# A hybrid attention and mixture-of-experts layer on one core: the shared gather moved between the halves of gate and up, left columns first, fewer steps before the first expert

## What is computed

```
logits = h @ router_w + router_b;  top 4 of 32 per token, softmax over them -> combine
for e in range(32):
    gate = min(h @ w_gate[e] + b_gate[e], 7)
    up   = clip(h @ w_up[e] + b_up[e], -7, 7)
    act  = gate * sigmoid(1.702 * gate) * (up + 1)
    y   += combine[:, e] * (act @ w_down[e] + b_down[e])
x = x + y;  final RMS norm
```

## Time and profile before

| what | value |
|---|---|
| median of three runs | 1249.69 us (1244.88 to 1253.77) |
| profiled execution | 1244.24 us, span 1242.5 us |
| TensorE matmul busy | 1156.3 us, 93% of the span |
| weight loading on TensorE | 606.0 us |
| VectorE, ScalarE, GpSimd busy | 355.5, 224.1, 9.1 us |
| read from HBM | 446.33 MB, 360 GB/s over the span |
| the ring's 384 loads | 128 each of gate, up, down; 26.5 to 26.9 us from issue to landing |

### The profile page before, as it was taken

How to read it: one execution, slowest core, us unless ns; L and a number is a source line. 1 busy time by engine, 2 the same in 40 slices (tenths; PEclk the granted TensorE clock), 3 DMA queues, 4 the chain that set the end, 5 groups by cost and what they waited for, 6 DMA issues and landing times.

```text
span 1242.5 us, 16294 instructions
## 1 busy us (share of the span) xinstructions
PE 1156.3 (93%) x6235; PEld 606.0 (49%) x6235; DVE 355.5 (29%) x768; ACT 224.1 (18%) x389; POOL 9.1 (1%) x16
## 2 busy tenths in 40 slices
PE   7999998898999999999999989898889989898987
PEld 6998998885344343434334333334333434343423
DVE  4446666443213221222221212212121212121212
ACT  5444446432001010101101000001010101010102
POOL 0000000000000000000000000000000000000000
PEclk9999999899999999999999999999999999999999
DMA  9956444568999999999999999999999999999992
GB/s 293 285 171 186 140 139 150 199 245 333 424 421 421 421 421 421 421 421 421 419 420 421 421 421 421 421 421 421 421 420 421 420 422 420 422 421 421 421 418 92
DMA packets 88916, 448.56 MB, mean 361 GB/s; under 512 B 7832, under 2 KB 35790, under 8 KB 39686
## 3 DMA queue, kind: packets, MB, share of 16 engines
q1 hardware_dynamic: 86282, 439.94, 87.3%
q0 software_dynamic: 1472, 5.51, 1.8%
q10 hardware_dynamic: 1084, 2.02, 0.5%
HBM read 446.33 MB, written 1.11 MB: 360 GB/s over the span
## 4 chain that ended last, share of the span: by engine, by line
PE 59%; DMA 37%; issue 1%; DVE 1%; SPq 1%; ACT 1%; ACTq 0%; DVEq 0%
DMA slot<-in_w_up 35%; PE psum L976 19%; PE psum L1005 9%; PE psum L667 5%; PE psum L668 5%; PE psum L669 5%; PE psum L919 4%; PE psum L934 3%; PE psum L942 2%; PE psum L977 2%; PE psum L737 1%; PE psum L772 1%; PE psum L765 1%; SPq L373 1%; PE psum L750 1%
## 5 line engine op out<-in xcount | busy, mean ns | idle before, releaser
L976 PE MATMUL psum<-slot,xT 128*64 128x512 f32 x1024 | 455.8, 597 | 58.0 <-DMA slot<-in_w_up 52.1
L977 PE MATMUL psum<-slot,xT 128*64 128x512 f32 x1024 | 457.2, 598 | 1.5 <-issue 1.5
L976 PEld LDWEIGHTS psum<-slot,xT 128*64 128x64 f32 x1024 | 136.6, 138 | 344.1 <-issue 344.1
L1005 PE MATMUL psum<-slot,guT 128*64 128x512 f32 x1024 | 233.8, 598 | 0.0
L1291 DVE COPY gu<-psum 128x512 f32<-128x512 f32 x32 | 22.1, 691 | 542.0 <-PE psum L977 542.0
L977 PEld LDWEIGHTS psum<-slot,xT 128*64 128x64 f32 x1024 | 136.6, 137 | 15.4 <-issue 15.4
L1005 PEld LDWEIGHTS psum<-slot,guT 128*64 128x64 f32 x1024 | 67.8, 136 | 129.1 <-issue 119.6
L639 ACT COPY gu<-psum 128x512 f32<-128x512 f32 x32 | 18.7, 585 | 466.4 <-PE psum L977 466.4
L1054 DVE TENSOR_TENSOR pieces<-raw,pieces 128x2048 fp32r<-128x2048 f32 x32 | 73.3, 2292 | 72.4 <-ACT pieces L474 72.4
L667 PE MATMUL psum<-hT_hi,pieces 128*128 128x256 f32 x296 | 84.9, 287 | 0.0
L668 PE MATMUL psum<-hT_lo,pieces 128*128 128x256 f32 x296 | 83.9, 284 | 0.0
(11 more groups left out here) (177 smaller groups left out, 945.3 us busy)
## 6 DMA issues: line engine op xcount, KB each, us to landing
slot<-in_w_gate SPq DMA_DIRECT2D x128, 1024.0 KB, 26.5
slot<-in_w_up SPq DMA_DIRECT2D x128, 1024.0 KB, 26.9
slot<-in_w_down SPq DMA_DIRECT2D x128, 1024.0 KB, 26.9
raw<-in_w_in SPq DMA_DIRECT2D x23, 1024.0 KB, 5.4
raw<-in_w_branch_a SPq DMA_DIRECT2D x4, 1024.0 KB, 5.0
raw<-in_w_out SPq DMA_DIRECT2D x4, 1024.0 KB, 4.9
windows<-bias_table POOLq DMA_DIRECT2D x8, 384.0 KB, 4.0
windows<-bias_table POOLq DMA_DIRECT2D x4, 576.0 KB, 7.1
```

The source lines that it names most:

```text
L976: mm(bank(GU + nb)[0:CAP, :], x_k, gate[:, c, cols], start=k == 0, stop=k == KC - 1)
L977: last = mm(bank(GU + nb)[CAP:P, :], x_k, up[:, c, cols], start=k == 0, stop=k == KC - 1)
L1005: last = mm(bank(DOWN)[half * CAP:(half + 1) * CAP, :], hidden[:, k, :], down[:, c, half * BANK:(half + 1) * BANK], start=k == 0, stop=k = ...
```

## The change

Parts, in the order of the program:

1. SyncE waits for `gu_rows_in` before it issues the third portion of expert weights.
2. VectorE no longer clears `y_half` and `spreadT` between building `pick` and the weights; GpSimd does, when the output projection is done. Three comparisons for the number of passes become one against a small table `limits`.
3. TensorE turns the combine weights into bank DOWN, after ScalarE has copied the left half of the gather, and waits for `weightT_done` only before the first expert's down, no longer before it reads the number of passes.
4. In the last quarter of gate and up, all left columns are done before the right ones, so `gu_half` is signalled two of four blocks before the end of the quarter and not one.
5. In the second expert of a pair the gather of the next pair stands after two of the four quarters of gate and up. ScalarE's `copy_gathered` waits until all gate and up of that expert is done, since it overwrites `xT`.
6. The last turn of ten experts is written out on SyncE and TensorE behind a loop of two; its very last load (the last quarter of the last down) comes in two halves with a semaphore each.

```diff
@@ sync
+            sp.wait_ge(gu_rows_in, 32)
             load_tenth(2)
...
-            with sp.Fori(0, TURNS) as i:
+            with sp.Fori(0, TURNS - 1) as i:
                 load_turn(0, i)
+            load_turn(0, TURNS - 1, final=True)
@@ sync, load_turn
-                        load(n, e)
+                        if final and n == HEAD * LOADS + TURN_LOADS - 1:
+                            for half in range(2):
+                                c = slice(half * ROWS // 2, (half + 1) * ROWS // 2)
+                                sp.dma_start(slot[n % RING][:, c, :], weights_of[2][e, PARTS - 1].rearrange(
+                                    "p (c n) -> p c n", c=ROWS)[:, c, :]).then_inc(last_in[half], 16)
+                        else:
+                            load(n, e)
@@ gpsimd
+            pool.wait_ge(x2_up, TT)
+            nc.gpsimd.memset(y_half[:, :], 0.0).then_inc(y_copied, 1)
+            nc.gpsimd.memset(spreadT[:, :], 0.0).then_inc(spreadT_done, 1)
@@ scalar
-            nc.scalar.copy(weightT[:, :], bank(GU)[0:E, 0:S]).then_inc(weightT_done, 1)
+            nc.scalar.copy(weightT[:, :], bank(DOWN)[0:E, 0:S]).then_inc(weightT_done, 1)
...
                         if odd:
+                            act.wait_ge(used, it * LOADS + 2 * PARTS)
                             copy_gathered(pair + 1)
@@ tensor, step
-                    for c in range(ROWS):
+                    inner = [(c, nb) for c in range(ROWS) for nb in range(2)]
+                    if h == PARTS - 1:
+                        inner = [(c, nb) for nb in range(2) for c in range(ROWS)]
+                    for c, nb in inner:
...
+                    if odd and h == PARTS // 2 - 1:
+                        pe.wait_ge(y_copied, it + 1)
+                        pe.wait_ge(spreadT_done, it + 1)
+                        gather(pair + 1)
...
-                if odd:
-                    gather(pair + 1)
+                if first:
+                    pe.wait_ge(weightT_done, 1)
...
+                    halved = last and h == PARTS - 1
...
+                        if halved and c % (ROWS // 2) == 0:
+                            pe.wait_ge(last_in[c // (ROWS // 2)], 16 * (p + 1))
@@ tensor, before the first expert
+            pe.wait_ge(xT_half, 1)
             for tt in range(TT):
-                last = tr(bank(GU)[0:E, tt * P:(tt + 1) * P], weights[:, tt, :], ident)
+                last = tr(bank(DOWN)[0:E, tt * P:(tt + 1) * P], weights[:, tt, :], ident)
             last.then_inc(weightT_up, 1)
             pe.wait_ge(passes_done, 1)
-            pe.wait_ge(weightT_done, 1)
@@ vector
-            v.memset(y_half[:, :], 0.0).then_inc(y_copied, 1)
-            v.memset(spreadT[:, :], 0.0).then_inc(spreadT_done, 1)
...
-            for p in range(1, PASSES):
-                step(v.tensor_scalar(few[0:1, 8 + p:9 + p], few[0:1, 8:9], float(CAP * p), None, ALU.is_gt))
+            step(v.tensor_scalar(few[0:1, 9:8 + PASSES], limits[0:1, :], few[0:1, 8:9], None, ALU.is_lt))
```

More of the change, by code:

```diff
@@ L163, in build @@
         unused = place("unused", [P, 4])
+        limits = place("limits", [1, PASSES - 1])
         at_rows = here[0]
@@ L274, in build @@
         slot_in = [sem(f"slot_in{i}") for i in range(RING)]
+        last_in = [sem(f"last_in{i}") for i in range(2)]
         used = sem("used")
@@ L302, in arrivals @@
         def arrivals(i):
-            return len(range(i, PASS_LOADS, RING))
+            return len(range(i, PASS_LOADS - 1, RING))
         def last_before(n):
@@ L373, in load, with load_turn @@
                 sp.dma_start(slot[i][:, :, :].rearrange("p c n -> p (c n)"), src).then_inc(slot_in[i], 16)
-            def load_turn(before, i):
+            def load_turn(before, i, final=False):
                 for k in range(TURN_EXPERTS):
@@ L952, in add_down_bias, with step @@
                            down_bias[:, nb * BANK:(nb + 1) * BANK], start=False, stop=False, skip_group_check=True)
-            def step(p, e, n0, later, bias=False):
+            def step(p, e, n0, later, first=False, last=False, bias=False):
                 it = p * E + e
@@ L1018, in _, with turn @@
                 for e in range(HEAD):
-                    step(p, e, e * LOADS, 0, bias=e == HEAD - 1)
-                with pe.Fori(0, TURNS) as i:
+                    step(p, e, e * LOADS, 0, first=e == 0, bias=e == HEAD - 1)
+                def turn(i, final=False):
                     for k in range(TURN_EXPERTS):
-                        step(p, i * TURN_EXPERTS + (HEAD + k), (HEAD + k) * LOADS, i * (TURN_LOADS // RING))
+                        step(p, i * TURN_EXPERTS + (HEAD + k), (HEAD + k) * LOADS, i * (TURN_LOADS // RING),
+                             last=final and k == TURN_EXPERTS - 1)
+                with pe.Fori(0, TURNS - 1) as i:
+                    turn(i)
+                turn(TURNS - 1, final=True)
             pe.wait_ge(y_copied, n_passes * E + 1)
@@ L1209, in _ @@
             v.memset(rank[:, :, :], FAR)
+            for p in range(1, PASSES):
+                v.memset(limits[:, p - 1:p], float(CAP * p))
             dve.wait_ge(moe_in, 48)
```

22 lines of the change are left out of this document (11 added, 11 removed).

## The result

| what | value |
|---|---|
| median after | 1234.52 us (1233.5 to 1235.57, 5 runs) |
| median before, same chip | 1247.06 us (1244.25 to 1253.77, 5 runs) |
| ratio | 0.9893, interval 0.986 to 0.9925 |
| profiled execution after | 1234.34 us, span 1232.1 us (before 1242.5) |

The change is faster by 1.1%, and the interval lies on both sides of 1%. The forecast of 1239.0 was 4.5 us too high; its range holds the time. Span against span the gain is 10.4 us, where the sum said 10.7. That they agree so well is partly luck: two terms were too small, and two losses were not in the sum (1.7 us at the router, and 0.65 us by which branch B began later).

What follows compares the result with a forecast made beforehand. DMA engines set the time in the experts, at the pace of the slowest engine. 5.2 + 0.7 + 2.3 + 2.5 = 10.7 us off 1249.7 gave 1239.0 us, range 1231.5 to 1246.

Steps and rivals of the forecast that it cites:

- the sum: Whole kernel: front, head, last expert and written-out turn, 5.2 + 0.7 + 2.3 + 2.5 = 10.7 us gained.
- Front, 5.2 us: Before the turning of gu_rows: the early wait removes 2.5 us of idle and 2.6 us of lowered clock.
- with it the fall of the clock: Branch B behind the gu_rows idle: without that idle the clock no longer falls, 2.6 us.
- What is late next is nothing up to the gather: From front to gather: everything is released by TensorE's progress and moves with it, so no gain is lost.
- Head, 0.7 us: Before the first expert: TensorE reads the number of passes after its own turning, 0.7 us gained (0 to 1.0).
- nothing waited for it: 0: Head of the experts: VectorE's result was ready before TensorE's turning of the weights, so dropping its steps gains 0.
- Last expert, 2.3 us: Last expert: the gather disappears in idle time, down starts 5.1 us after the turning, not 7.43; bounds 0 and 4.0.
- Written-out turn, 2.5 us: Weight stream: no second branch back on SyncE, 3.5 instruction fetches of 0.73 us saved; 0 to 3.7 us.
- Steady experts, 0: Other experts: the moved gather and a 1.6 us wait for ScalarE's copy cost 0, since the stream covers them.
- It holds: Second expert: the stream's cover suffices, as gaps of 7.4 and about 9 us are shorter than 12.4.
- The rival of the dry ring: Second experts of pairs: late down releases stop the DMA engines; slower, 1259 or up to 1299 us; chance 0.04.
- Left columns and the load in halves, 0: Gate and up's last quarter and the last down load: left columns 0 to 0.2 us, taken as 0; halves 0.

Runs made afterwards that it cites:

- e6: Changed kernel without SyncE's wait for gu_rows before the third portion of expert weights; 1238.62 us, ratio 0.9918.
- e1: The changed kernel run again without an edit, as base line; 1235.54 us, ratio 0.99 against the kernel before.
- e7: Changed kernel with TensorE's wait for weightT put back before it reads the number of passes; 1239.17 us, one run.
- e8: Changed kernel with VectorE's two clearings and three comparisons back as before; 1235.3 us, one run.
- e4: Changed kernel with the gather back behind the turning, before down; 1236.19 us, ratio 0.9904.
- e2: Changed kernel with SyncE's last turn back in its loop and the last load whole, TensorE's turn still written out; 1239.06 us, ratio 0.9932.
- e3: Changed kernel with all three turns written out on SyncE; 1235.46 us, ratio 0.9904.
- e9: Kernel before with only SyncE's wait for gu_rows ahead of the third portion added; 1241.84 us, ratio 0.9938.
- e12: Changed kernel with early copy of gathered tokens, down biases in the 23rd expert, SyncE's turns all written out, three router fillers instead of four; 1230.97 us, ratio 0.9857.
- e5: Changed kernel with ScalarE copying the gathered tokens ahead of both sigmoids, once gate and up are done; 1233.78 us, ratio 0.988.
- e11: e5 with the down bias products moved from the second expert to the 23rd; 1233.52 us, ratio 0.9872.

## Why the prediction was right or wrong

1. **Front, 5.2 us: right in the first profile, too large in most.** 5.0 within the branch, 4.4 at the router. The 2.5 us of idle time are gone in all twelve profiles with the wait and back in e6. The 2.6 us of clock are gone in four; in eight a short fall is left, and the branch gains 3.5 to 3.8 us. The step "with it the fall of the clock" is the weak one, and so is its reason, that idle times up to 2.1 us left the clock at its level: in e1 the clock fell behind one of 1.98 us. That the profiled execution had no fall there is luck. "What is late next is nothing up to the gather" failed: the router's filler cost 1.7 us at half clock, so 2.7 us reached the gather. That loss comes and goes with the execution (e1 hasn't got it).
2. **Head, 0.7 us: mechanism right, size wrong by three.** Measured 2.1 (e7). I moved the register read from 299.03 to TensorE's turning and left its 1.41 us on the path. But the read doesn't have to follow the last matmul: it fits beside the gather (e7). I also bounded the term at 1.0, below what a read that costs nothing would have given. VectorE's steps, "nothing waited for it: 0", are worth 0.4 (e8): the cover that I named was TensorE's turning, and the change removed that cover.
3. **Last expert, 2.3 us: right,** 2.4, with the wait on ScalarE at 1.50 (forecast 1.6). The medians, 0.65 us apart (e4), can't confirm it; what the second expert gives back may be in them.
4. **Written-out turn, 2.5 us: mechanism right, somewhat too small.** 3.2 in the stretch, 3.5 by e2, five packets and not three and a half. The Trainium skill (Runtime: NRT & Kernel Launch, Instruction fetch mechanics) says that a taken branch to a target outside the two pages at hand forces a fetch; the cluster goes and comes back with the branch (18, 13 and 18 packets in the stream). The same section says that the streaming of instructions is mostly hidden; the time here changed by 3.5 us with the written-out turn, so for this kernel the measurement decides. That seven *more* packets could be dropped for no gain (e3) I had not foreseen: the step that was missing is to ask how far the second-slowest DMA engine is behind the slowest.
5. **Steady experts, 0: right from the third on, not quite in the second.** "It holds" rested on down at full clock; at half clock SyncE's gap was 10.1 us instead of 9 and the rate dipped, as it did in every profile whose clock fell in that expert. The rival of the dry ring had its seed here, but in one expert out of fifteen and at a price of one or two microseconds, not 60.
6. **Left columns and the load in halves, 0:** from down to the end nothing moved (17.99 and 17.98 us, and 17.95 in e2 without the halves), and from the fourth quarter to the turning it takes 3.59 us before and after. The left columns were not tried alone, nor was TensorE's turn written out.
7. **The median.** I took the sum from the median of three runs, 1249.69. Beside the changed kernel the old one had 1247.06, so 2.6 of the 4.5 us too many were in that starting point. The medians also differ by more (12.5) than the profiled executions do (10.4 in span); e9, whose one line was forecast at 5.2, gave 7.0. The mean granted clock that each run's record holds points at the reason. Of the 33 runs of the kernel before beside the experiments, the three at 0.993 or more took 1244.1 to 1244.6 us and the six at 0.986 or less 1250.2 to 1255.6, with 0.989 as the median. The profiled execution of that kernel, at 0.993, belongs to the fast ones, while 0.993 is the median of the changed kernel's eleven runs. So the old kernel's typical execution seems to spend more time at half clock than its profiled one, and the change to remove some of that as well. Where in the kernel it does so no profile shows.

## What to carry to other kernels

When a step is moved, ask what its result's reader has queued in front of it: here the gather moved well, and one copy on ScalarE, moved as far, gave the other 1.5 us. When a wait in front of a register read or a branch is taken away, price the whole latency of the read as hidden, and look at once at what was hidden behind the old wait. Read the clock from several executions before you count on it. And where a weight stream sets the time, count the instruction fetches that lie in it: they cost no engine any time that its row shows, and the branch that went with five of them was over a quarter of this change (3.5 of 12.9 us by the medians of e2 and e1). Look at the end of the stream too: how long one DMA engine works alone there bounds what dropping them can give.

## What the runs showed of the hardware that I had not expected

- The granted clock fell while TensorE was busy without a gap: 0.61 on the mean of 283 to 287 us in the changed kernel after the router's products of 32 columns, 0.66 in 345 to 350 after bias products with 32 rows, 0.51 for 7 us in e12, and 0.52 in 225 to 228 in e5, behind the 32x32 turning of `gu_rows`. Before it fell TensorE had been busy, but on narrow tiles. When the bias products were elsewhere (e11), it didn't fall there. That the narrow tiles are the cause is not shown: in other executions it stayed at 1.00 behind the same products (the router in e1, the second expert before).
- Where it falls varies between executions of one kernel: near 14, 89, 284 and 345 us in the first profile, near 15, 90, 202 and 346 in e1. An idle time of 1.98 us near 200 us was followed by a fall in e1 and by none in the kernel before.
- A register read of 1.41 us on TensorE lies wholly beside the matmuls in front of it, if no wait for their copied result stands between them (4.24 against 6.33 us from gather to first expert).
- A transfer of `gu_rows` that queued with 2 MB of weights ended an idle time of 3.53 us (e6); issued ahead of them it ended none.
- SyncE's last branch back, with five fetch packets of 18, was worth 3.5 us; dropping seven more was worth nothing.
- The 16 DMA engines don't end the stream together: the share is 0.06, one engine, from 1220 to 1224 us before, and 0.50 two microseconds before the end in e3.
